# Redealing the filler matmuls between the ten levels of a recurrence on TensorE

## The reference, cut to what matters

```python
qf = silu(q) * KDIM ** -0.5
f  = lower_bound + (1 - lower_bound) * sigmoid(f_raw);  k = 1 - f
# S_t = diag(f_t) S_{t-1} + k_t i_t^T ;   o_t = S_t^T q_t      (causal)
o  = o * rsqrt(mean(o * o) + EPS) * out_norm * silu(g)
```

## Time and profile before

| | us |
|---|---|
| median of 3 runs | 763.84 (762.19 to 766.01) |
| the profiled execution | 763.84 |
| its span (first to last instruction) | 762.1 |

### The profile page before, as it was taken

One profiled execution on the slowest core, in us unless ns is written; L12 is line 12 of the kernel. 1 busy time (PEld: TensorE's weight loads), 2 busy tenths in 40 slices (PEclk: granted clock), 3 DMA queues, 4 the chain that ended last, 5 costly groups with the idle time before them and its releaser, 6 DMA issues.

```text
span 762.1 us, 11054 instructions
## 1 busy us (share of the span) xinstructions
PE 715.5 (94%) x3962; PEld 557.9 (73%) x3962; DVE 440.0 (58%) x813; ACT 297.4 (39%) x478; POOL 15.5 (2%) x47
## 2 busy tenths in 40 slices
PE   4999999999998898699969999999999999999995
PEld 3665477777676686578858888888888878888884
DVE  4967688889999988743484233333332236343434
ACT  6444453554435343322584432344334313121223
POOL 6000000000000000000000000000000000000000
PEclk9899999999999999889999999999999999999999
DMA  9943122222215776415112445543353223323202
GB/s 316 357 132 83 28 57 75 65 83 60 63 45 157 231 248 220 138 56 194 56 56 59 134 138 138 138 126 97 95 150 110 83 88 134 100 93 98 68 0 111
DMA packets 95850, 89.10 MB, mean 117 GB/s; under 512 B 2934, under 2 KB 84938, under 8 KB 95820
## 3 DMA queue, kind: packets, MB, share of 16 engines
q1 hardware_dynamic: 95820, 88.70, 38.2%
HBM read 86.59 MB, written 2.10 MB: 116 GB/s over the span
## 4 chain that ended last, share of the span: by engine, by line
PE 76%; DVE 14%; issue 4%; ACT 4%; DMA 1%; SPq 0%; DVEq 0%; ACTq 0%
PE ps L1302 44%; PE ps L1323 21%; DVE act L862 2%; DVE w_lo L801 2%; PE ps L1510 1%; DMA act<-in_w_ada 1%; PE ps L1403 1%; PE ps L1592 1%; PE ps L1535 1%; ACT w_hi L459 1%; PE ps L1574 1%; DVE act L1125 1%; DVE act L1123 1%; PE ps L1411 1%; DVE act L1122 1%
## 5 line engine op out<-in xcount | busy, mean ns | idle before, releaser
L1302 PE MATMUL ps<-h_hi,w_hi 128*128 128x512 f32 x576 | 235.3, 409 | 1.4 <-DVE h_lo L880 1.4
L1302 PE MATMUL ps<-h_hi,w_lo 128*128 128x512 f32 x576 | 225.5, 391 | 0.0
L1302 PE MATMUL ps<-h_lo,w_hi 128*128 128x512 f32 x576 | 225.3, 391 | 0.0
L801 DVE TENSOR_TENSOR w_lo<-w_raw,w_hi 128x1024 fp32r<-128x1024 f32 (+1 forms) x110 | 130.4, 1187 | 114.2 <-ACT w_hi L459 114.0
L459 ACT ACTIVATE w_hi<-w_raw 128x1024 fp32r<-128x1024 f32 (+1 forms) x110 | 112.7, 1029 | 112.0 <-PE ps L1323 91.7
L1302 PEld LDWEIGHTS ps<-h_hi,w_hi 128*128 128x128 f32 x576 | 108.8, 189 | 33.4 <-issue 11.2
L1302 PEld LDWEIGHTS ps<-h_hi,w_lo 128*128 128x128 f32 x576 | 108.6, 188 | 23.2
L1302 PEld LDWEIGHTS ps<-h_lo,w_hi 128*128 128x128 f32 x576 | 108.9, 189 | 22.0 <-issue 1.5
L1323 PE MATMUL ps<-w_hi,h_hi 128*128 128x512 f32 x240 | 94.4, 393 | 9.4 <-DVE h_lo L808 7.3
L1323 PE MATMUL ps<-w_lo,h_hi 128*128 128x512 f32 x240 | 93.9, 391 | 0.0
L1323 PE MATMUL ps<-w_hi,h_lo 128*128 128x512 f32 x240 | 93.9, 391 | 0.0
(11 more groups left out here) (231 smaller groups left out, 703.5 us busy)
## 6 DMA issues: line engine op xcount, KB each, us to landing
w_raw<-in_w_ffn_in SPq DMA_DIRECT2D x44, 512.0 KB, 5.6
w_raw<-in_w_in SPq DMA_DIRECT2D x28, 512.0 KB, 3.9
w_raw<-in_w_ffn_out SPq DMA_DIRECT2D x22, 512.0 KB, 3.5
adaw<-in_w_ada SPq DMA_DIRECT2D x12, 512.0 KB, 4.1
act<-in_w_ada SPq DMA_DIRECT2D x12, 512.0 KB, 9.2
adaw<-in_w_ada SPq DMA_DIRECT2D x6, 1024.0 KB, 5.3
act<-in_w_ada SPq DMA_DIRECT2D x6, 1024.0 KB, 5.3
res<-in_x SPq DMA_DIRECT2D x8, 512.0 KB, 4.7
```

The lines of the kernel that those rows point to most:

```text
L801: V.tensor_tensor(w_lo[slot][:, 0:n], w_raw[slot][:, 0:n], w_hi[slot][:, 0:n].bitcast(f32), ALU.subtract).then_inc(lo_ok, 1)
L1302: last = mm(ps[bank][0:rows, :], a, b, start=(k == 0 and n == 0), stop=(k == KT - 1 and n == 2))
```

## The change

The product `q_f = q * f` moves behind level 0: level 0 now reads `q_f` before it is multiplied in place, and `q_raw` is no longer written by DVE. On PE the transposes of `i` and three projection steps go ahead of level 0, and the 31 steps are dealt out as three ahead, three behind each of levels 0 to 7, and two behind each of levels 8 and 9 (in the last body these become 2, 2, 2, 3, 2, 2, 2, 3, 2 and 1, 2). On DVE the twelve search rounds and the four splits are dealt out anew over the levels. On ACT the sigmoid of the next head goes ahead of the slot 2 split. All amounts of work stay as they are.

```diff
@@ top
-LEVEL_STEPS = (0, 5, 3, 5, 2, 4, 4, 3, 3, 2)
-LEVEL_ROUNDS = ((0,), (), (1, 2), (), (3, 4), (5,), (6,), (7, 8), (9,), (10, 11))
@@ ACT, hg_f
-                if not (isinstance(hh, int) and hh == 0):
-                    split_hi(2, hh + U_HG[2], hh * 4 + (G_HG - 1))
                 sc.wait_ge(group_done, hh * 4 + (G_HG + 1))
                 if not (isinstance(hh, int) and hh == 0):
                     sc.wait_ge(raw_taken, hh)
                 sc.activation(f_, ps[1][:, :], ACT.Sigmoid).then_inc(f_sig, 1)
+                if not (isinstance(hh, int) and hh == 0):
+                    split_hi(2, hh + U_HG[2], hh * 4 + (G_HG - 1))
@@ DVE, hg_body
-                V.scalar_tensor_tensor(out=q_raw, in0=q_raw, scalar=float(HEAD ** -0.5), in1=q_sig, op0=ALU.mult,
+                V.scalar_tensor_tensor(out=q_f, in0=q_raw, scalar=float(HEAD ** -0.5), in1=q_sig, op0=ALU.mult,
                                        op1=ALU.mult).then_inc(lvl_ready, 1)
-                ve.wait_ge(lvl_ready, h * LEVELS + 1)
-                V.tensor_tensor(q_f, q_raw, f_w, ALU.mult).then_inc(lvl_ready, 1)
...
                     ve.wait_ge(lvl_mm, h * LEVELS + (st + 1))
-                    if 0 < st < LEVELS - 1:
+                    if st == 0:
+                        V.tensor_tensor(q_f, q_f, f_w, ALU.mult).then_inc(lvl_ready, 1)
+                    elif st < LEVELS - 1:
...
-                    rounds = LEVEL_ROUNDS[st]
+                    rounds = ((0,), (), (1,), (2, 3), (4,), (5, 6), (7,), (8, 9), (10,), (11,))[st]
...
                     if isinstance(h, int) and h == HG_HEADS - 1:
-                        if st in (1, 4, 9):
-                            split_lo(*{1: (G_ATT + 1, 1), 4: (G_ATT + 2, 2), 9: (G_ATT + 3, 0)}[st])
-                    elif st in (1, 3, 6, 8):
-                        at, slot = {1: (5, 1), 3: (6, 2), 6: (7, 3), 8: (8, 0)}[st]
+                        if st in (0, 3, 9):
+                            split_lo(*{0: (G_ATT + 1, 1), 3: (G_ATT + 2, 2), 9: (G_ATT + 3, 0)}[st])
+                    elif st in (0, 2, 5, 9):
+                        at, slot = {0: (5, 1), 2: (6, 2), 5: (7, 3), 9: (8, 0)}[st]
                         split_lo(h * 4 + (G_HG + at), slot)
@@ PE, hg_body
-                    q = q_f if st else q_raw
...
-                def project(n, count):
+                def project(n):
                     if last_head:
-                        att_project(0, n * 24 // 32, (n + count) * 24 // 32)
+                        att_project(0, n * 24 // 32, (n + 3 if n < 27 else n + 2) * 24 // 32)
                     else:
-                        hg_project(h + 1, n, n + count)
-
-                level(0)
-                level(1)
+                        hg_project(h + 1, n, n + 3 if n < 27 else n + 2)
+
                 te.wait_ge(i_raw, h + 1)
                 for t in range(TT):
                     last = nc.tensor.transpose(ps[6][:, t * P:(t + 1) * P], i_t[:, t * P:(t + 1) * P], ident[:, :])
                 last.then_inc(iv_mm, 1)
-                for st in range(1, LEVELS):
-                    if st > 1:
-                        level(st)
-                    project(sum(LEVEL_STEPS[:st]), LEVEL_STEPS[st])
+                project(0)
+                for st in range(8):
+                    level(st)
+                    project(3 + 3 * st)
+                level(8)
+                project(27)
+                level(9)
+                project(29)
```

More of the change, by code:

```diff
@@ L1535, in level @@
                                 last = mm(bank[32 * j:32 * j + 32, t * 32:(t + 1) * 32], k_b[:, at:at + 32],
-                                          q[:, at + ahead:at + ahead + 32], start=True, stop=True)
+                                          q_f[:, at + ahead:at + ahead + 32], start=True, stop=True)
                     elif st == 7:
```

## The result

The changed kernel takes 771.55 us in the median of eight executions, the kernel before 763.87. One of the changed kernel's eight took 1787.16 us, for which nothing here gives a reason, and the ratio is of the fast runs alone (15 of the changed kernel, with a median of 770.25), so that it isn't the quotient of those two medians. It is 1.0075, 95% interval 1.0045 to 1.0104, so +5.7 us (3.4 to 7.9); the prediction was +4.7 and 768.5. The profiled execution took 771.73 with a span of 769.9, against 762.1 before.

A forecast was written before the change was run, and what follows sets the result against it. DVE's chain was taken to bound the bodies, despite PE's high matmul busy time. Bodies 0 to 3 add 0.9 + 1.4 + 1.4 + 1.0 = +4.7 us to 763.84, giving 768.5; range 763 to 772.

The forecast's parts named there:

- DVE's chain, not PE, ends a body: Recurrence bodies: DVE's summed blocks set level 9's time; bodies 0 to 2 lengthen by 0.9, 1.4 and 1.4 us.
- The first rival: Bodies: PE sets the time, DVE keeps up, waits and clock loss go; -3.4 us, 760.4; chance 0.12.
- the sum of blocks: DVE's level blocks in body 1 added from S+3.2: 23.3 us, update 9 at S+26.5, body 33.75 against 32.37.
- The hoist makes DVE start later than it can make good: Body start: DVE begins level work at S+3.2, not S+0.75, and recovers only later idle time, 0.64 and some 0.9 us.
- Two levels alone instead of a pair: PE, levels 0 and 1 of each body: standing alone they cost 0.39 to 0.46 us more PE time.
- One round more ahead of level 9's update: DVE's search: 10 of 12 rounds precede level 9's update, 9 before, adding a 256-column round of 0.73 us.
- The product behind level 0: DVE, level 0 block: the product with f (L1062) moves behind level 0, same instruction, same 0.61 us.
- ACT's order: Sigmoid ahead of slot 2 split: taken at 0, margin 0.3 us; 1.0 us a body if a table load intervened.
- The clock in body 3: A fall likelier than not after a 2.2 us wait at level 5, +0.9; body 3 taken at +1.0 us.

The follow-up runs named there:

- e4: Changed kernel with the top-k search on 16 columns only, so the key selection isn't computed; ratio to the kernel before 0.9959.
- e8: Changed kernel, ACT's order undone, search rounds 0 and 1 and first split ahead of level 0's wait, later rounds moved up; ratio to before 0.9992.
- e9: Kernel before with the changed kernel's dealing of rounds and splits, and search round 0 ahead of the wait for level 0; 760.60 us, ratio 0.9950.
- e5: Kernel before with only the transposes and three projection steps put ahead of the pair of levels 0 and 1; ratio to before 1.0090.
- e2: Kernel before with only DVE's search rounds and splits dealt over the levels as in the changed kernel; ratio to before 0.9972.
- e7: Changed kernel with the product q*f back ahead of level 0, which reads q_raw again; ratio to the kernel before 1.0067.
- e1: Changed kernel with ACT doing the slot 2 split ahead of the next head's sigmoid again; ratio to the kernel before 1.0085.
- e6: Kernel before with only ACT's order changed, the sigmoid ahead of the slot 2 split; ratio to before 0.9981.
- e3: Changed kernel with DVE's rounds and splits back at the levels of the kernel before; ratio to the kernel before 1.0194.

## Why the prediction was right, and which terms were off

*The forecast as a whole.* It was for 768.5 us; the measured ratio on its 763.84 gives 769.6. The mechanism holds and one term was mis-sized, as the items below say.

*DVE's chain, not PE, ends a body.* Right. e4 takes work off DVE alone and the bodies shrink; e8 moves that work and they reach PE's floor. The first rival (PE sets the time, 760.4) had as its evidence the 98% busy PE, and that share told nothing: in the changed kernel PE is still 94% busy in body 1. Nor does the other pair of shares decide it (weight loads 73% and DVE 90% in body 1 before): body 1 of e8 has 73% and 91%, body 1 of e9 75% and 92%, and in both PE sets the time. What decides is whether DVE's updates come before PE's next level, which the sum of blocks answered and no share does.

*The hoist makes DVE start later than it can make good.* Right. DVE began at S+3.15 for 3.2, and e5, the hoist alone, loses most of what the change loses: at full clock 5.0 us of 6.6. Body 0 was put at +0.9 and came to +1.10.

*Two levels alone instead of a pair.* 0.39 to 0.46 against 0.46 (e4) and 0.47 (e8).

*One round more ahead of level 9's update, named as part of the loss.* Half right. It stands in the changed kernel's chain, but the dealing as a whole gains: e2 is faster than the kernel before, since it lets DVE swallow ACT's delay at the tail. I summed this correctly inside the bodies and didn't see that it was a gain standing alone.

*The product behind level 0.* Put in DVE's block at 0.61, right in the sum, but little of a loss by itself: e7 gets less than 0.1 a body back in bodies 0 to 2, and in body 3 0.44, against e1.

*The step that was mis-sized: ACT's order, taken at 0 with a margin of 0.3 us.* The margin assumed the table load to be done before the wait. It stood behind it, 1.28 us, and the split came 0.84 us late. That case was priced at 1.0 us a body in the text; e1 measures 0.94 and 0.93 by undoing it. Bodies 1 and 2 at 34.60 and 34.56 are the 33.75 of the sum plus this; e1's 33.66 and 33.63 are the sum's number without it (its last steps, 27.4 + 6.31, add to 33.71). Against the sum, bodies 1 and 2 are 1.6 too long together, body 0 0.2 too long and body 3 0.4 too short, which is the gap between the 4.7 foreseen and the 6.1 measured.

*The clock in body 3, taken as likelier to fall than not.* Wrong in the profiled execution: after 2.06 us of waiting it stayed at 1.00 (there was a fall in e1 and e7, at the same place after the same wait). The term was 1.0, between 0.5 and 1.4, and came to 0.59. The chain on DVE was right both ways: S+29.05 without a fall, measured 29.19, and 29.95 with the 0.9 for one, measured 29.89 in e1. The last steps of that sum, 26.35 + 2.55, give 28.90 and not 29.05. But the S+28.6 of before, against which it was set, had a fall in it; without one the kernel before would be at about 28.13, by e6, so at equal clock the change costs 1.06 in body 3. With a fall in body 3 the total would have been 6.8 us instead of 6.1 (29.89 in place of 29.19), so that it came as near to the 4.7 is in part luck.

## What to carry to other kernels

Work that is put ahead of the first link of a round-trip chain delays every later link on the other engine; here it became free only when that engine was given something to do in the meantime that it would have done inside the chain (e8 against e1). Before an operation is moved ahead of another on an in-order engine, count what its wait will hold back with it, a table load among them: the same move was free in e6 and cost 0.9 us a body behind a later releaser. And when a bundle loses, time its parts alone: here the part that looked like a cost was the one worth keeping.

## What the runs showed of the hardware that was not expected

The granted clock did not follow from the wait. After the same instructions and a wait of 1.99 and 2.00 us, it fell in body 1 of e5 and not in body 2, which is 35.71 - 34.13 = 1.58 us; after 1.70 us it fell in the kernel before and after 1.66 not in e6; after 2.06 not in the changed kernel and after 2.07 in e1. After 3.37 us in e3 it fell both times. What decides behind waits of this length was not settled here. The same goes for PE's next long wait, in the attention behind body 3: after 2.69 us the clock over the next 4 us was 1.00 in the kernel before and 0.59 in e6. Differences of 1.5 us between two profiles can be this alone, which is why the bodies are compared and not the spans, and each with its clock.

A table load was held by one wait and not by the other. In body 0 of the kernel before the sigmoid's load ran at 108.82 and the sigmoid then waited for PE until 111.35; in the changed kernel the load itself waited 3.94 us for DVE's `g_w`. The code waits for PE's `group_done` first and for `raw_taken` second. The load stands behind the second and not behind the first in e5 too, where one sigmoid shows both: in body 0 its load waited 1.00 us for `g_w` and ran at 110.17, and the sigmoid itself then waited 0.40 us more for PE. Whether the order of the two waits in the code decides this was not tried.
